# A first mixer whose steps stand in another order on TensorE, ScalarE and VectorE

## The reference

```python
def first_block(x, ...):
    h = rms_norm(x, attn_norm_g[l])
    proj = jnp.einsum('bsd,de->bse', h, w_in[l])
    qa, ka, va, qb, kb, vb, f_logit, g_logit = jnp.split(proj, bounds, axis=-1)
    o_a = merge_heads(moba_attention(qa, ka, va))        # q, k normalised and rotated
    o_b = merge_heads(forgetting_attention(qb, kb, vb, log_f))
    merged = gates[:, :, 0] * (o_a @ w_branch_moba[l]) + gates[:, :, 1] * (o_b @ w_branch_fox[l])
    x = x + merged @ w_out[l]
    h2 = rms_norm(x, ffn_norm_g[l])
    u, g = jnp.split(h2 @ w_ffn_up[l], 2, axis=-1)
    g = causal_depthwise_conv(g, ffn_conv_w[l], ffn_conv_b[l])
    x = x + (jax.nn.silu(g) * u) @ w_ffn_down[l]
def second_block(x, mem, ...):                            # mem_n @ w_kv is needed here
    ...
def reference(...):                                       # second_block(first_block(x), mem)
```

## Time and profile before

| | before |
|---|---|
| median of 3 runs | 734.34 us (733.11, 734.34, 734.57) |
| profiled execution | 732.7 us, of it 730.9 us span |
| PE busy | 716.3 us, 98% of the span, 4460 matmuls |
| PE loading weights (PEld) | 617.0 us, 84% |
| DVE busy | 511.1 us, 70%, 792 instructions |
| ACT busy | 451.9 us, 62%, 694 instructions |
| loaded by DMA | 127.95 MB, 175 GB/s in the mean |

### The profile page before, as it was taken

The page is one execution under the profiler, slowest core; times in us unless marked ns, Lnnn a source line. Parts: engine busy times, 40 slices in busy tenths (PEclk is TensorE's granted clock), DMA queues, the critical chain, the costliest instruction groups (busy, mean ns, idle before and its releaser), DMA issues.

```text
span 730.9 us, 11816 instructions
## 1 busy us (share of the span) xinstructions
PE 716.3 (98%) x4460; PEld 617.0 (84%) x4460; DVE 511.1 (70%) x792; ACT 451.9 (62%) x694; POOL 8.4 (1%) x18
## 2 busy tenths in 40 slices
...
GB/s 333 239 273 125 241 145 159 130 146 158 160 144 195 180 175 206 193 175 202 255 214 177 124 169 86 127 113 145 69 192 215 242 188 155 169 209 217 228 102 30
DMA packets 70463, 127.95 MB, mean 175 GB/s; under 512 B 4915, under 2 KB 17172, under 8 KB 70420
## 3 DMA queue, kind: packets, MB, share of 16 engines
...
HBM read 126.30 MB, written 1.05 MB: 174 GB/s over the span
## 4 chain that ended last, share of the span: by engine, by line
PE 81%; ACT 7%; DVE 6%; DMA 4%; issue 2%; SPq 1%; ACTq 0%; DVEq 0%
PE acc L607 19%; PE acc L609 18%; PE acc L608 18%; PE acc L599 6%; PE acc L600 6%; PE acc L601 6%; DVE b_wlo L1562 2%; ACT b_whi L1069 2%; DMA b_raw<-in_w_in 1%; PE banks L629 1%; PE banks L642 1%; DMA b_gates<-in_mem 1%; PE banks L659 1%; DMA b_raw<-in_w_out 1%; DMA b_raw<-in_w_ffn_in 1%
## 5 line engine op out<-in xcount | busy, mean ns | idle before, releaser
L1562 DVE TENSOR_TENSOR b_wlo<-b_raw,b_whi 128x1024 fp32r<-128x1024 f32 (+4 forms) x232 | 269.0, 1187 | 97.3 <-ACT b_whi L1069 96.1
L1069 ACT ACTIVATE b_whi<-b_raw 128x1024 fp32r<-128x1024 f32 (+4 forms) x232 | 231.6, 1027 | 92.0 <-PE acc L609 30.9
L607 PE MATMUL acc<-b_whi,b_hhi 128*128 128x512 f32 (+4 forms) x480 | 186.1, 388 | 0.3 <-DVE b_hqT L2010 0.3
L609 PE MATMUL acc<-b_wlo,b_hhi 128*128 128x512 f32 (+4 forms) x480 | 181.0, 377 | 0.0
L608 PE MATMUL acc<-b_whi,b_hlo 128*128 128x512 f32 (+4 forms) x480 | 180.9, 377 | 0.0
L607 PEld LDWEIGHTS acc<-b_whi,b_hhi 128*128 128x128 f32 x480 | 90.2, 188 | 18.3 <-issue 2.5
L609 PEld LDWEIGHTS acc<-b_wlo,b_hhi 128*128 128x128 f32 x480 | 90.2, 188 | 14.9
L608 PEld LDWEIGHTS acc<-b_whi,b_hlo 128*128 128x128 f32 x480 | 90.3, 188 | 13.2
L599 PE MATMUL acc<-b_ohi,b_whi 128*128 128x256 f32 x352 | 99.9, 284 | 1.6 <-DVE b_olo L1595 1.5
L600 PE MATMUL acc<-b_olo,b_whi 128*128 128x256 f32 x352 | 99.6, 283 | 0.0
L601 PE MATMUL acc<-b_ohi,b_wlo 128*128 128x256 f32 x352 | 99.6, 283 | 0.0
...
## 6 DMA issues: line engine op xcount, KB each, us to landing
...
```

Source lines behind the costliest of these rows:

```text
L607: nc.tensor.matmul(o, a, wh, start=first, stop=False)
L609: mm = nc.tensor.matmul(o, a, wl, start=False, stop=last)
L1069: ins = A(whi[:, n % SPLIT, 0:c["nk"], 0:c["n"]], raw[:, n % RAW, 0:c["nk"], 0:c["n"]], ACT.Copy)
L1562: ins = V.tensor_tensor(wlo[:, n % SPLIT, 0:c["nk"], 0:c["n"]], raw[:, n % RAW, 0:c["nk"], 0:c["n"]], whi[:, n % SPLIT, 0:c["nk"], 0:c["n" ...
```

## The change

Only the three lists of `ORDER1` change. `ORDER2`, the instructions, their shapes and the bytes that are loaded stay as they were. The file has one line less, so line numbers of `after` are one lower than those of `before` behind the table. One change in the order of chunks follows: the twelfth to fourteenth (counted from 0: 11, 12, 13) were `va 1, ka 2, ka 3` and are now `ka 2, ka 3, va 1`. In the diff `("gemm", "ka", 2, 0)` is chunk 2 of `ka` for tile 0, and a gemm entry with no tile does both.

```diff
 ORDER1["pe"] = [...
-     ("gemm", "ka", 0), ("gemm", "ka", 1, 0), ("gemm", "va", 0, 0), ("gemm", "ka", 1, 1), ("gemm", "ka", 2, 0),
-     ("gemm", "va", 0, 1), ("gemm", "va", 1, 0), ("gemm", "va", 2, 0), ("turn", "mk"), ("gemm", "ka", 3, 0),
+     ("gemm", "ka", 0), ("gemm", "ka", 1, 0), ("gemm", "ka", 2, 0), ("gemm", "va", 0, 0), ("gemm", "va", 1, 0),
+     ("gemm", "ka", 1, 1), ("gemm", "va", 0, 1), ("turn", "mk"), ("gemm", "va", 2, 0), ("gemm", "ka", 3, 0),
...
-     ("gemm", "kb", 1, 1), ("gemm", "kb", 2, 1), ("probs", 0), ("gemm", "kb", 3, 1), ("scores", 2), ("pv", 0),
+     ("gemm", "kb", 3, 0), ("probs", 0), ("gemm", "kb", 2, 1), ("gemm", "kb", 3, 1), ("scores", 2), ("pv", 0),
...
-     ("gemm", "vb", 1, 0), ("probs", 2), ("gemm", "fg2", 2, 1), ("gemm", "fg2", 3, 1), ("turn", "kb"),
-     ("gemm", "vb", 1, 1), ("scores", 4), ("pv", 2), ("gemm", "vb", 2, 0), ("probs", 3), ("gemm", "vb", 3, 0),
+     ("gemm", "vb", 1, 0), ("gemm", "fg2", 2, 1), ("gemm", "fg2", 3, 1), ("turn", "kb"), ("gemm", "vb", 1, 1),
+     ("probs", 2), ("scores", 4), ("pv", 2), ("gemm", "vb", 2, 0), ("probs", 3), ("gemm", "vb", 3, 0),
...
-     ("norm turn", "ffn1", 1, 0), ("gemm", "wo1_1", 3, 1), ("gemm", "s1", 0, 0), ("gemm", "s1", 1, 0),
-     ("gemm", "s1", 0, 1), ("norm turn", "ffn1", 1, 1), ("gemm", "s1", 1, 1), ("gemm", "s1", 2), ("gemm", "s1", 3)]
+     ("norm turn", "ffn1", 1, 0), ("gemm", "wo1_1", 3, 1), ("gemm", "s1", 0, 0), ("gemm", "s1", 0, 1),
+     ("norm turn", "ffn1", 1, 1), ("gemm", "s1", 1, 0), ("gemm", "s1", 1, 1), ("gemm", "s1", 2), ("gemm", "s1", 3)]
 ORDER1["act"] = [...
-     ("guess", "qa"), ("turn", "mk"), ("vectors", 0), ("hi", "fg0", 0), ("sums", "va", 0), ("sums", "ka", 0, 1),
+     ("sums", "ka", 0, 1), ("hi", "fg0", 0), ("vectors", 0), ("sums", "va", 0), ("hi", "fg0", 1), ("guess", "ka"),
...
-     ("gate log", "fg4"), ("hi", "brb1", 1), ("pv", 6), ("hi", "wo1_1", 0), ("probs", 7), ("mix", 3),
-     ("hi", "wo1_0", 1), ("pv", 7), ("mix", 4), ("hi", "wo1_0", 3), ("merged hi", 0, 0), ("hi", "wo1_0", 2),
+     ("hi", "brb1", 1), ("pv", 6), ("hi", "wo1_1", 0), ("probs", 7), ("mix", 3), ("pv", 7), ("mix", 4),
+     ("hi", "wo1_0", 3), ("hi", "wo1_0", 2), ("merged hi", 0, 0), ("merged hi", 0, 1), ("merged hi", 1, 0),
...
 ORDER1["dve"] = [...
-     ("norm sum", "ffn1", 1, 0), ("norm gain", "ffn1", 1, 0), ("lo", "s1", 1), ("norm lo", "ffn1", 0, 0),
-     ("norm sum", "ffn1", 1, 1), ("norm lo", "ffn1", 0, 1), ("norm gain", "ffn1", 1, 1), ("norm lo", "ffn1", 1, 0),
-     ("lo", "s1", 2), ("norm root", "ffn1"), ("norm lo", "ffn1", 1, 1), ("lo", "s1", 3)]
+     ("lo", "s1", 1), ("norm gain", "ffn1", 0, 0), ("norm sum", "ffn1", 0, 1), ("norm gain", "ffn1", 0, 1),
+     ("norm sum", "ffn1", 1, 0), ("norm gain", "ffn1", 1, 0), ("norm lo", "ffn1", 0, 0), ("norm lo", "ffn1", 0, 1),
+     ("norm sum", "ffn1", 1, 1), ("norm gain", "ffn1", 1, 1), ("norm lo", "ffn1", 1, 0), ("norm root", "ffn1"),
+     ("norm lo", "ffn1", 1, 1), ("lo", "s1", 2), ("lo", "s1", 3), ("lo", "wo1_1", 3)]
```

More of the change, by code:

```diff
@@ L90 @@
 ORDER1, ORDER2 = {}, {}
[L91 to L94, removed]
+ORDER1["pe"] = [("norm turn", "mem", 0, 0), ("norm turn", "mem", 1, 0), ("norm turn", "mem", 0, 1),
+     ("gemm", "mkv", 0, 0), ("norm turn", "mem", 1, 1), ("gemm", "mkv", 1, 0), ("gemm", "mkv", 0, 1),
+     ("gemm", "mkv", 1, 1), ("gemm", "mkv", 2, 0), ("gemm", "mkv", 3, 0), ("norm turn", "x1", 0, 0, 1),
+     ("gemm", "mkv", 2, 1), ("gemm", "mkv", 3, 1), ("norm turn", "x1", 1, 0), ("gemm", "qa", 0), ("gemm", "qa", 1, 0),
```

30 lines of the change are left out of this document (14 added, 16 removed), and 50 rows, old and new, of the table pick.

## The result

| | before | after |
|---|---|---|
| median, first series | 734.46 us (4 runs) | 730.14 us (4 runs: 729.42 to 730.88) |
| profiled execution, span | 732.7, 730.9 us | 730.41, 728.6 us |
| PE busy in the first mixer, of 228 us | 222.17 us | 224.19 us |

The ratio is 0.9945 (95% interval 0.9929 to 0.996), 4.0 us faster; the medians lie 4.3 us apart. Two later series of the unchanged after, on two chips, gave 0.9972 (0.9958 to 0.9985, 12 runs) and 0.9954 (0.9938 to 0.9969, 9 runs). The three intervals hold 0.9958 to 0.996 in common, 2.9 to 3.1 us.

A forecast was written before the change was run, and what follows sets the result against it. PE was taken as the bound; terms -1.55 - 0.25 - 0.39 - 0.40 - 0.30 + 0.40 = -2.5 us took the profiled 732.7 to 730.2 us. With 1.64 us up to the median: 731.9 us, range 730.5 to 734.3.

The forecast's parts named there:

- Parts 1 and 2: End of the first mixer: stops ahead of `s1 0 0` and `s1 2 0` shrink, gains 1.55 and 0.25 us.
- Parts 3 and 4: PE's waits at `probs 0` (for `divide 0`) and `scores 4` (for `turn kb`) go, gains 0.39 and 0.40 us.
- Part 5: PE's wait at `brb0 1 0` goes as ACT's hi moves behind the copy, gain 0.30 us.
- Part 6: Near 41 us: late los delay `va 1 0`, and `heads mk` delays `turn mk`; loss 0.4 us, bounds 0 to 1.0.
- Parts 7 and 8: 46 to 66 us (hi's behind `sums ka 0 1`) and output projection (`merged hi 0 0`): loss 0 in both.
- Rivals B and C: B (0.10): ACT stuck in `sums ka`, +1.5 us, median 735.8. C (0.10): stops reappear one step on, net 0, median 734.3.
- A: New waits at five places with little slack give back 1.2 us; net -1.3 us, median 733.0, chance 0.20.
- ceiling: Most an order can win from PE's stops in the first mixer: about 2.8 us by brackets, 3.1 by starts.
- rival E: Granted clock: removing these short stops gives nothing back by it, a new stop might cost it; no chance given.

The follow-up runs named there:

- twelve_more: after with twelve more 512-column matmuls on PE at the first step of qb; 732.50 us, ratio 0.9986 to before.
- end_back_2: after with the end of the mixer in before's order, a second time, on one chip with a series of after; 732.33 us, ratio 0.9977 to before.
- end_only: before with only the end of the mixer in the order of after; 732.29 us, ratio 0.9968 to before.
- end_back: after with the end of the mixer in the order of before; ratio 0.9973 to before.
- after_again: after with no edit, run again (12 runs); 731.87 us, ratio 0.9972 to before.
- probs7_first: after with ACT's copies of probs 7 ahead of the hi of wo1_1's first chunk, and the hi of brb1 0 ahead of them; ratio 0.9966 to before.
- early_back: after with the first 66 us in the order of before on all three engines; 731.52 us, ratio 0.9954 to before.
- best: after with the edits of early_back and filled, plus ACT's probs 7 and pv 7 copies and merged hi 0 0 moved earlier; 728.10 us, ratio 0.9922 to before.
- filled: after with 14 more 128-column transposes on PE in the second mixer, where it waits; 729.17 us, ratio 0.9945 to before.

## Why the prediction was wrong, point by point

**What bounds the kernel: right.** PE does, and an us of PE is an us at the end: in the trace of twelve_more, and by 2.25 us for 2.1 in the timed runs of end_back_2.

**Parts 1 and 2, the end: right, a little small.** Forecast 1.55 and 0.25 us, measured 1.69 and 0.38, alone (end_only), undone (end_back) and undone on one chip with after (2.25 us in time).

**Parts 3 and 4, probs 0 and scores 4: right in mechanism, too small.** I took the brackets of the rows, 0.39 and 0.40 us. From start to start the steps had 0.53 and 0.56 us too much. A bracket counts from the modelled end of the matmul before, which lies past the regular start of the next by some 0.17 us. VectorE in after has `divide 0` ahead of the maxima, as said, 4.4 us ahead of `probs 0` at 90.68:

```profile
86.28 1.01 DVE L1682 TENSOR_SCALAR b_xn<-b_xn,b_rc 128x256 f32<-128x256 f32 x4
87.20 0.42 DVE L1664 CUSTOM_DVE_ANT_0 b_Sm<-banks,b_cst 128x256 f32<-128x256 f32 x1
```

**Part 5, brb0 1 0: half right.** That wait went, but ScalarE's hi ahead of `probs 7` waits for its load, and PE now waits one step earlier. After:

```profile
172.27 1.06 ACT L1068 ACTIVATE b_whi<-b_raw 128x1024 fp32r<-128x1024 f32 x1 [1.33 <-DMA b_raw<-in_w_out]
173.23 0.47 ACT L1170 ACTIVATE b_PT<-banks 128x384 f32<-128x384 f32 x1
```

```profile
174.19 0.40 PE L687 MATMUL banks<-b_PT,b_v 128*64 128x256 f32 x1 [0.28 <-ACT b_rp L1170]
```

`pv 7` and `brb0 1 0` together had 0.63 and 0.55 us too much in the traces of before and 0.53, 0.18 and 0.38 in those of after: a gain of 0.23 in the mean for the 0.30 forecast. All five hold the 0.17 us of `pv 7` that is no stop.

**Part 6, the new place near 41 us: right size, other route.** `va 1 0` did not wait. ScalarE's chain ran as worked out, but the hi's behind that of chunk 12 then waited for their loads, and `heads mk` stood behind all four los. In after, then in after_again:

```profile
35.08 1.07 ACT L1068 ACTIVATE b_whi<-b_raw 128x1024 fp32r<-128x1024 f32 x1 [1.68 <-DMA b_raw<-in_w_in]
36.05 0.67 ACT L1099 ACTIVATE b_qraw<-acc,b_rs 128x512 f32<-128x512 f32 x1
...
38.70 1.04 ACT L1068 ACTIVATE b_whi<-b_raw 128x1024 fp32r<-128x1024 f32 x1
...
41.44 1.06 ACT L1068 ACTIVATE b_whi<-b_raw 128x1024 fp32r<-128x1024 f32 x1 [0.35 <-DMA b_raw<-in_w_in]
42.84 1.06 ACT L1068 ACTIVATE b_whi<-b_raw 128x1024 fp32r<-128x1024 f32 x1 [0.34 <-DMA b_raw<-in_w_in]
```

```profile
43.93 1.23 DVE L1561 TENSOR_TENSOR b_wlo<-b_raw,b_whi 128x1024 fp32r<-128x1024 f32 x1 [0.17 <-ACT b_whi L1068]
...
46.40 0.69 DVE L1653 TENSOR_TENSOR b_qraw<-b_qraw,b_hgain 128x512 f32<-128x512 f32 x1
```

```profile
38.39 4.75 DVE L1561 TENSOR_TENSOR b_wlo<-b_raw,b_whi 128x1024 fp32r<-128x1024 f32 x4 [2.37 <-ACT b_whi L1068]
...
44.38 0.69 DVE L1653 TENSOR_TENSOR b_qraw<-b_qraw,b_hgain 128x512 f32<-128x512 f32 x1
```

In after_again the four los ran in one go (4.75 us) and the last multiplication of `heads mk` ended at 45.07, in time; in after it ended at 47.09 and `turn mk` started at 47.14. The stop was 0.45, 0 and 0.46 us in the three traces, 0.5 to 0.85 in four of the five traces of kernels made from after with its first part, none in the fifth (probs7_first), and never there in early_back and best. I had taken 0.4.

**Parts 7 and 8: right**, no stop between 50 and 66 us or at the output projection in any trace of after. Rivals B and C did not come; of A came two places, `turn mk` and `pv 7`, with 0.45 and 0.36 us in after (0.53 less the 0.17), none in after_again, and not the 1.2.

**The sum.** 2.5 us forecast; from `qa` to `s1` the traces of after have 2.6, 3.5 and 2.6 us less than the mean of the two of before (198.87), 2.9 in the mean; with filled, 2.1 us less, it is 2.7. The predicted 731.9 us met the second series (731.87), where before itself stood at 734.17, and missed the first and the third (729.99).

**The step that failed** is the one from the trace to the median: "The median of the runs shown, 734.34, lies 1.64 us above it, so the median comes to 731.85". The sum of the stops held, and the worked-out profiled execution of 730.2 us met 730.41. But the 1.64 us did not carry over: the median of after, 730.14, lies 0.27 us *below* its own profiled execution. No stop explains that; the timed runs of before lay well above its profiled one, those of after did not.

The range made the same mistake: "from the ceiling, 734.34 - 3.1 = 731.2, less 0.7 us for the scatter of the three runs". In the pair of the first series the order gained 2.6 us, below the ceiling, which brings 734.34 to 731.7; the measured median is 1.6 us below that, more than twice the 0.7 allowed. Three runs within 1.5 us said little on the scatter: twelve runs of before span 4.2 us. The traces show two things that differ between executions: `qa` starts between 22.1 and 25.0 us, and the clock near 520 us, which I had named (rival E) but only for new stops and not as something that changes from run to run. How much each adds to a single time was not taken apart, and for the timed runs of before in the first series neither is on record, so the cause of their 1.64 us stays open.

The ceiling was too small as well. It took `probs 0` and `scores 4` by their brackets; by starts it is 0.53 + 0.56 + 0.46 + 1.69 + 0.38 = 3.6 us, and best, in which PE waits nowhere, has 3.9 us less than before. With 3.9 the range would have begun at 729.7 and held 730.14, but by luck: after did not reach that ceiling.
